# Thirty-two of 88 gate and up tile pairs computed by seven half-width block products instead of eight

## The chip, the cores and the metric

The kernel runs on one core of a Trainium2 chip. The metric is the time on the device, in microseconds (us), of one execution; the median of 3 runs is given. The core has a matrix engine (TensorE, PE in the profile; its weight loads are PEld), VectorE (DVE), ScalarE (ACT), GpSimd (POOL) and SyncE (SP), which here only issues the loads of the weights. Each engine works through its own queue in order and waits on semaphores.

## The reference, cut to what matters

A two-layer network over 512 tokens of width 1024, all float32, then a hybrid mixer and a mixture of experts. Four times in it (two layers, two places each) stands a feed-forward block of hidden width 2816:

```python
def swiglu(h, w_gate, w_up, w_down):
    return (jax.nn.silu(h @ w_gate) * (h @ w_up)) @ w_down

x = x + 0.5 * swiglu(rms_norm(x, norm_w[i, 0]), ffn_w_gate[i, 0], ffn_w_up[i, 0], ffn_w_down[i, 0])
```

## The kernel before, in words

Everything is held transposed: 128 features on the partitions, 512 tokens along the free axis. The stages run in the order ffn00, ssm, ffn01, ffn10, mla, ffn11, mixer, moe; the four that begin with ffn are the blocks above. A float32 product is made from rounded parts: a matrix `a` is split into `a_hi` (rounded) and `a_lo` (the rest), and hi\*hi, hi\*lo and lo\*hi are added up in one PSUM bank, three matmuls of 512 columns for a 128x128 block of weights (`block`, L254 to L256).

A **unit** is eight such blocks of weights (128x1024 numbers, 512 KB). SyncE loads unit `u` into slot `u % 4` of `raw` (in the profile `w_lo_exact`) as soon as TensorE is done with unit `u - 4` (`load_unit`, L224); GpSimd rounds it to `w_hi` (`split_pool`, L232); VectorE makes `w_lo` (`split_vector`, L246); TensorE runs 24 matmuls of 512 columns.

An ffn stage has two halves. A half has eleven **pairs** j = 0 to 10 (`HALF_FF`), each one gate unit and then one up unit, and then eleven units of the down projection, eight output tiles `m` of eleven blocks each. For a pair VectorE scales the gate's sum by the inverse rms (`act`, L738), ScalarE applies silu (L702), VectorE multiplies by the up sum (`prod`, L763), ScalarE rounds the product (`g_hi`, L717), VectorE makes `g_lo` (L770). The hidden product of pair j - 1 and the splits of pair j + 1 are made while TensorE works on pair j. The order of each engine's work is written out by hand, in `ffn_tensor`, `ffn_scalar` and `ffn_vector`, pair by pair.

At the start of a stage ScalarE computes the inverse rms (L318, L320), loads the table for silu (L698) and only then comes to the silu of pair 0. In ffn01 and ffn10 the ScalarE queue also issues, per pair, the load of a piece of another weight (`mod_load`, L798), which waits until VectorE has added the piece before (`mod_add`, L807, two operations per pair).

Of the kernel before, what the change touches and what calls it, by code (L numbers as in the profile page):

```python
# [62 lines left out]
for shared, names in (("lru scalar", ("w hi by scalar", "lru u", "lru gate a", "lru gate x", "lru a", "lru a2", "lru tanh", "root", "gelu")),  # L63
                      ("lru vector", ("lru margin", "lru conv", "log a", "gated x", "one less a2", "lru", "lam", "decay rate", "csp", "slopes")),
# [96 lines left out]
def plan(k):  # L161
# [80 lines left out]
def split_vector(k, u):  # L242

    if u < len(k.units):
        k.ve.wait_ge(*k.at("w hi by scalar" if u in k.by_scalar else "w hi", u))
        k.ve.tensor_tensor(k.w_lo[:, u % SLOTS, :], k.raw[:, u % SLOTS, :], k.w_hi[:, u % SLOTS, :].bitcast(F32), ALU.subtract).then_inc(*k.up("split", u))  # L246


def block(k, u, b, bank, x, first, stop):
# [3 lines left out]
    hi, lo = k.w_hi[:, u % SLOTS, span(b)], k.w_lo[:, u % SLOTS, span(b)]  # L253
# [351 lines left out]
def ffn_tiles(k, with_mod):  # L605
    k.base = k.mod_end_at if with_mod else k.stage_at
    k.g_hi = k.sb("g_hi", [P, HALF_FF, T], F32R)
    k.g_lo = k.sb("g_lo", [P, HALF_FF, T], F32R)
    k.act = k.sb("act", [P, T])
    k.prod = k.sb("prod", [P, T])  # L610
    if with_mod:
        k.mod_w = k.sb("mod_w", [P, 2, 512])
# [11 lines left out]

def ffn_sync(k, stage):
    for u in range(k.unit_at[stage], k.unit_at[stage] + 2 * HALF_UNITS):
        load_unit(k, u)


def ffn_pool(k, stage):  # L630
    u0 = k.unit_at[stage]
# [51 lines left out]

def ffn_scalar(k, stage, mod_tiles=None):
    ae = k.ae
    for half in range(2):
        u0, down = ffn_units(k, stage, half)
        for j in range(HALF_FF):
            if mod_tiles:
# [22 lines left out]
def gate_hi_scalar(k, stage, half, j, down):  # L712
# [4 lines left out]
    ae.activation(k.g_hi[:, j, :], k.prod[:, :], ACT.Copy).then_inc(*k.up("g hi", (stage, half, j)))  # L717


def ffn_vector(k, stage, mod_tiles=None):  # L720
    ve = k.ve
    for half in range(2):
        u0, down = ffn_units(k, stage, half)
        for j in range(HALF_FF):
            if j:
# [23 lines left out]
        for d in range(HALF_FF):  # L749
            split_vector(k, down + d + 2)  # L750
# [6 lines left out]
def gate_prod_vector(k, stage, half, j, u0):  # L757
    ve = k.ve
    ve.wait_ge(*k.at("unit", u0 + 2 * j + 1))
# [3 lines left out]
    ve.tensor_tensor(k.prod[:, :], k.act[:, :], k.bank[UP_BANKS[j % 2]][:, :], ALU.mult).then_inc(*k.up("prod", (stage, half, j)))  # L763


def gate_lo_vector(k, stage, half, j):
# [3 lines left out]
    ve.tensor_tensor(k.g_lo[:, j, :], k.prod[:, :], k.g_hi[:, j, :].bitcast(F32), ALU.subtract).then_inc(*k.up("g lo", (stage, half, j)))  # L770
# [2735 lines left out]
```

## Time and profile before

| | |
|---|---|
| time, median of 3 runs | 2695.33 us (2695.09 to 2696.34) |
| profiled execution, from its first to its last instruction | 2692.5 us |
| matmuls | 12738, TensorE busy 98% |
| VectorE busy | 1632.1 us, 61% |
| ScalarE busy | 869.7 us, 32% |
| GpSimd busy | 653.6 us, 24% |
| mean granted TensorE clock | 0.996 |

The profile gives no other time of that execution than its span, which lies 2.8 us under the median of the runs. A matmul's duration in the profile contains the way through the pipeline, so successive matmuls overlap; what a matmul costs in a dense stretch is the distance from its start to the start of the next. The same holds, by a smaller overlap, for ScalarE and VectorE.

### The profile page before, as it was taken

What the parts mean: (1) busy time and instruction counts of PE and PEld (TensorE: products, weight loads), DVE (VectorE), ACT (ScalarE), POOL (GpSimd) and SP (SyncE); (2) the same over time, 40 slices, a digit from 0 to 9 for tenths busy, and PEclk for the clock granted to TensorE, in tenths of its full rate; (3) what the DMA queues carried; (4) which work ended last, traced back from release to release, by engine and by line L of the source; (5) the groups of instructions that cost most, each with busy time, mean ns of one, the idle gap of its engine ahead of it and who ended that gap; (6) DMA issues with size and microseconds to landing.
All of it is one profiled execution on the core that took longest, in us unless ns stands there. A gap on an engine that the chain in (4) does not pass through costs nothing.

```text
span 2692.5 us, 32765 instructions
## 1 busy us (share of the span) xinstructions
PE 2635.1 (98%) x12738; PEld 2184.7 (81%) x12738; DVE 1632.1 (61%) x2391; ACT 869.7 (32%) x1501; POOL 653.6 (24%) x700
## 2 busy tenths in 40 slices
PE   8999999999999999999999999999999999899998
PEld 6888887778778888888888889988888878777886
DVE  5344468988846545565455657754343477768996
ACT  3101125666611101121001135621001035537995
POOL 2111221222322211221211247722211141012220
PEclk9999999999999999999999999999999999999999
DMA  4333333333324434445445330023333364037995
GB/s 124 98 94 101 95 94 107 96 105 102 94 81 138 141 111 147 133 118 148 125 128 146 104 106 2 9 71 101 94 98 98 92 82 64 15 125 281 373 368 228
DMA packets 457067, 325.80 MB, mean 121 GB/s; under 512 B 34657, under 2 KB 421042, under 8 KB 456658
## 3 DMA queue, kind: packets, MB, share of 16 engines
q1 hardware_dynamic: 435240, 287.22, 36.3%
q10 hardware_dynamic: 15050, 28.08, 3.4%
q0 software_dynamic: 6624, 8.41, 0.9%
q8 instruction: 102, 1.67, 0.3%
q14 instruction: 51, 0.42, 0.0%
HBM read 323.06 MB, written 16.32 MB: 126 GB/s over the span
## 4 chain that ended last, share of the span: by engine, by line
PE 91%; DVE 5%; ACT 2%; DMA 1%; issue 1%; SPq 0%; POOL 0%; DVEq 0%; ACTq 0%; POOLq 0%
PE bank L254 24%; PE bank L256 24%; PE bank L255 24%; PE bank L1483 2%; PE bank L2953 2%; PE bank L2955 1%; PE bank L2954 1%; PE bank L1583 1%; PE bank L1777 1%; PE bank L1789 1%; PE bank L1551 1%; PE bank L2972 1%; PE bank L2974 1%; PE bank L2973 1%; PE bank L2936 1%
## 5 line engine op out<-in xcount | busy, mean ns | idle before, releaser
L254 PE MATMUL bank<-h_hi,w_hi 128*128 128x512 f32 x1992 | 789.6, 396 | 8.5 <-DVE w_lo L246 3.9
L256 PE MATMUL bank<-h_hi,w_lo 128*128 128x512 f32 x1992 | 776.4, 390 | 0.0
L255 PE MATMUL bank<-h_lo,w_hi 128*128 128x512 f32 x1992 | 775.9, 389 | 0.0
L232 POOL TENSOR_SCALAR w_hi<-w_lo_exact 128x1024 fp32r<-128x1024 f32 x325 | 361.9, 1113 | 1464.9 <-DMA w_lo_exact<-in_ffn_w_gate 390.5
L246 DVE TENSOR_TENSOR w_lo<-w_lo_exact,w_hi 128x1024 fp32r<-128x1024 f32 x369 | 455.1, 1234 | 145.1 <-POOL w_hi L232 133.4
L254 PEld LDWEIGHTS bank<-h_hi,w_hi 128*128 128x128 f32 x1992 | 374.2, 188 | 94.9 <-ACT h_hi L350 6.9
L255 PEld LDWEIGHTS bank<-h_lo,w_hi 128*128 128x128 f32 x1992 | 374.4, 188 | 79.3 <-issue 3.4
L256 PEld LDWEIGHTS bank<-h_hi,w_lo 128*128 128x128 f32 x1992 | 374.1, 188 | 78.7
L254 PE MATMUL bank<-g_hi,w_hi 128*128 128x512 f32 x704 | 273.9, 389 | 0.0
L255 PE MATMUL bank<-g_lo,w_hi 128*128 128x512 f32 x704 | 273.9, 389 | 0.0
L256 PE MATMUL bank<-g_hi,w_lo 128*128 128x512 f32 x704 | 273.9, 389 | 0.0
L702 ACT ACTIVATE act<-act 128x512 f32<-128x512 f32 x88 | 55.7, 633 | 629.1 <-DVE act L738 629.0
L738 DVE TENSOR_TENSOR act<-bank,norm_r 128x512 f32<-128x512 f32 x88 | 60.8, 691 | 258.5 <-PE bank L256 235.9
L763 DVE TENSOR_TENSOR prod<-act,bank 128x512 f32<-128x512 f32 x88 | 60.5, 687 | 235.0 <-PE bank L256 233.5
L717 ACT ACTIVATE g_hi<-prod 128x512 fp32r<-128x512 f32 x88 | 55.7, 633 | 402.5 <-DVE prod L763 402.5
L2871 DVE TENSOR_TENSOR e_lo<-e_lo_exact,e_hi 128x1024 fp32r<-128x1024 f32 x138 | 160.7, 1218 | 2.7 <-ACT e_hi L2865 2.7
L254 PEld LDWEIGHTS bank<-g_hi,w_hi 128*128 128x128 f32 x704 | 132.1, 188 | 27.5
L256 PEld LDWEIGHTS bank<-g_hi,w_lo 128*128 128x128 f32 x704 | 132.1, 188 | 27.5
L255 PEld LDWEIGHTS bank<-g_lo,w_hi 128*128 128x128 f32 x704 | 132.1, 188 | 27.3
L2865 ACT ACTIVATE e_hi<-e_lo_exact 128x1024 fp32r<-128x1024 f32 x138 | 138.6, 1060 | 0.9 <-ACT h_rows L3163 0.8
L388 ACT ACTIVATE h_hi<-x,cols 128x512 fp32r<-128x512 f32 x40 | 29.0, 725 | 248.5 <-DVE x L368 153.6
L366 DVE SCALAR_TENSOR_TENSOR norm_ht<-bank,norm_r 128x512 f32<-128x512 f32 x64 | 44.2, 690 | 103.8 <-PE bank L256 103.8
(490 smaller groups left out, 3830.5 us busy)
## 6 DMA issues: line engine op xcount, KB each, us to landing
w_lo_exact<-in_ffn_w_gate SPq DMA_DIRECT2D x88, 512.0 KB, 3.8
w_lo_exact<-in_ffn_w_up SPq DMA_DIRECT2D x88, 512.0 KB, 3.9
w_lo_exact<-in_ssm_w_in SPq DMA_DIRECT2D x48, 512.0 KB, 4.1
mod_w<-in_w_mod ACTq DMA_DIRECT2D x48, 512.0 KB, 3.8
e_lo_exact<-in_w_gate SPq DMA_DIRECT2D x46, 512.0 KB, 6.0
e_lo_exact<-in_w_up SPq DMA_DIRECT2D x46, 512.0 KB, 7.5
e_lo_exact<-in_w_down SPq DMA_DIRECT2D x46, 512.0 KB, 6.6
w_lo_exact<-in_ffn_w_down SPq DMA_DIRECT2D x32, 512.0 KB, 3.9
```

The lines of the kernel that those rows point to most:

```text
L232: ge.tensor_scalar(k.w_hi[:, u % SLOTS, :], k.raw[:, u % SLOTS, :], 1.0, 0.0, ALU.mult, ALU.add).then_inc(*k.up("w hi", u))
L246: k.ve.tensor_tensor(k.w_lo[:, u % SLOTS, :], k.raw[:, u % SLOTS, :], k.w_hi[:, u % SLOTS, :].bitcast(F32), ALU.subtract).then_inc(*k.up(" ...
L254: te.matmul(k.bank[bank][:, :], hi, x_hi, start=first, stop=False)
L255: te.matmul(k.bank[bank][:, :], hi, x_lo, start=False, stop=False)
L256: return te.matmul(k.bank[bank][:, :], lo, x_hi, start=False, stop=stop)
L702: ae.activation(k.act[:, :], k.act[:, :], ACT.Silu).then_inc(*k.up("act", (stage, half, j)))
L717: ae.activation(k.g_hi[:, j, :], k.prod[:, :], ACT.Copy).then_inc(*k.up("g hi", (stage, half, j)))
L738: ve.tensor_tensor(k.act[:, :], k.bank[GATE_BANKS[j % 2]][:, :], k.nr[:, :], ALU.mult).then_inc(*k.up("scaled gate", (stage, half, j)))
L763: ve.tensor_tensor(k.prod[:, :], k.act[:, :], k.bank[UP_BANKS[j % 2]][:, :], ALU.mult).then_inc(*k.up("prod", (stage, half, j)))
L1483: ins = te.matmul(to, w, x, start=m == 0, stop=m == len(terms) - 1)
L2865: ae.activation(k.e_hi[:, n % RING, :], k.e_raw[:, n % RING, :], ACT.Copy).then_inc(*k.up("expert hi", (b, i)))
L2871: ve.tensor_tensor(k.e_lo[:, n % RING, :], k.e_raw[:, n % RING, :], k.e_hi[:, n % RING, :].bitcast(F32), ALU.subtract).then_inc(*k.up("exp ...
```

## The change: what it does

Of the 22 pairs of each ffn stage some are now **joined**: in ffn00 and ffn11 the pairs 4, 6, 7, 9, 10 of the first half and 0, 1, 3, 4, 6, 7, 9, 10 of the second; in ffn01 and ffn10 the pairs 4, 6, 8 of the first half. That is 32 of 88. The others stay as they were.

A joined pair is seen as a 2x2 block product: gate and up are the two block rows, the upper and lower half of the 1024 inputs (four 128-blocks each) the inner index, the first and second 256 tokens the two block columns. It is computed by seven products instead of eight, by a scheme of the Strassen and Winograd family. Each product is 12 matmuls of 256 columns (four blocks, three terms). Three products have quarters of the weights as operands (`UP_1`, `UP_2`, `GATE_2`), four have sums of such quarters (`DIFF`, `SUM`, `SUM_LESS`, `SUM_LEAST`); on the other side stand halves of `h` or four sums of halves, `t`.

New work of VectorE for a joined pair: four sums of quarters (128x512), seven `operand_lo` (128x512), and seven 128x256 operations that put products together and make `prod` in two halves. It makes no 128x1024 splits for it. New work of ScalarE: seven `operand_hi` (128x512) and three copies of products (128x256) out of PSUM. GpSimd no longer rounds the two units of a joined pair. At the start of each ffn stage ScalarE makes `h_exact` (eight 128x512 operations with a scale by column) ahead of the silu of pair 0; in pair 1 VectorE makes four sums `t` and ScalarE their `t_hi` (128x1024 each), in pairs 2 and 3 VectorE makes three and one `t_lo`.

TensorE's order in a joined pair is `UP_1, DIFF, UP_2, SUM, GATE_2, SUM_LESS, SUM_LEAST`. `UP_2`, `GATE_2` and `SUM_LEAST` add onto the PSUM region of `UP_1`, `DIFF` and `SUM`, so each waits until ScalarE has copied that region. A pair now waits for `prod` of the pair two before it, ahead of its first matmul.

The core of the diff:

```diff
 def load_unit(k, u):
     se = k.se
-    if u >= SLOTS:
+    if u - SLOTS in k.joined_units:
+        for name, key in k.joined_units[u - SLOTS]:
+            se.wait_ge(*k.at(name, key))
+    elif u >= SLOTS:
         se.wait_ge(*k.at("unit", u - SLOTS))
...
+def joined_tensor(k, stage, half, j):
...
+    onto = {UP_2: UP_1, GATE_2: DIFF, SUM_LEAST: SUM}
+    for i in range(N_PRODUCTS):
+        te.wait_ge(*k.at("operand lo", (stage, half, j, i)))
+        if i in onto:
+            te.wait_ge(*k.at("copied", (stage, half, j, onto[i])))
...
+        for q in range(KH):
+            x_hi, x_lo = x_of[i](q)
+            te.matmul(out_of[i], hi[:, span(q)], x_hi, start=i not in onto and q == 0, stop=False, skip_group_check=True)
+            te.matmul(out_of[i], hi[:, span(q)], x_lo, start=False, stop=False, skip_group_check=True)
+            ins = te.matmul(out_of[i], lo[:, span(q)], x_hi, start=False, stop=q == KH - 1, skip_group_check=True)
...
+def operand_hi_scalar(k, stage, half, j, i):
...
+    if i in OF_SUMS:
+        ae.wait_ge(*k.at("operand sum", (stage, half, j, i)))
+        source = k.s_exact[:, lo_slot(stage, half, j, i), :]
+    else:
+        u = gate if i == GATE_2 else gate + 1
+        ae.wait_ge(*k.at(f"load {u % SLOTS}", u))
+        source = {UP_1: up_1, UP_2: up_2, GATE_2: gate_2}[i]
+    ae.wait_ge(*k.at(*k.entry_free[stage, half, j, i]))
+    ae.activation(operand_hi(k, stage, half, j, i), source, ACT.Copy).then_inc(*k.up("operand hi", (stage, half, j, i)))
```

ScalarE's queue for pair j (`then`: pair j + 1 is joined; `again`: pairs j and j - 1 are both joined):

```diff
             if (half, j) == (0, 0):
                 exp_tables(k)
                 inverse_rms_scalar(k, stage, D, 7)
                 ae.preload_act_table(ACT.Silu)
+                if stage == "ffn00":
+                    ae.wait_ge(*k.at("x", ("setup", KD - 1)))
+                for m in range(KD):
+                    ae.activation(k.h_exact[:, m, :], k.x[:, m, :], ACT.Copy, scale=gain(k, stage, m)).then_inc(*k.up("h exact", (stage, m)))
+            again = joined and j and is_joined(stage, half, j - 1)
+            if again:
+                operand_hi_scalar(k, stage, half, j, SUM_LESS)
+                ae.wait_ge(*k.at("joined", (stage, half, j - 1, "gate second")))
+                copy_product_scalar(k, stage, half, j, UP_1)
+                copy_product_scalar(k, stage, half, j, DIFF)
+                operand_hi_scalar(k, stage, half, j, SUM_LEAST)
+            if then:
+                operand_hi_scalar(k, stage, half, j + 1, UP_1)
+            if j and is_joined(stage, half, j - 1):
+                silu_scalar(k, stage, half, j - 1)
+            if joined and not again:
+                operand_hi_scalar(k, stage, half, j, SUM_LESS)
+            if j:
+                gate_hi_scalar(k, stage, half, j - 1, down)
...
+            if joined and not again:
...
+                copy_product_scalar(k, stage, half, j, UP_1)
+                copy_product_scalar(k, stage, half, j, DIFF)
+                operand_hi_scalar(k, stage, half, j, SUM_LEAST)
+            if joined:
+                copy_product_scalar(k, stage, half, j, SUM)
+            if then:
+                for i in (SUM, DIFF, UP_2, GATE_2):
+                    operand_hi_scalar(k, stage, half, j + 1, i)
+            if not joined:
+                silu_scalar(k, stage, half, j)
```

VectorE's queue for pair j begins:

```diff
+            if again:
+                operand_lo_vector(k, stage, half, j, SUM)
+                operand_sum_vector(k, stage, half, j, SUM_LEAST)
+                operand_lo_vector(k, stage, half, j, SUM_LESS)
+            if j and is_joined(stage, half, j - 1):
+                joined_rest_vector(k, stage, half, j - 1)
+            if then:
+                operand_sum_vector(k, stage, half, j + 1, SUM)
+            if again:
+                operand_lo_vector(k, stage, half, j, SUM_LEAST)
             if j:
                 gate_prod_vector(k, stage, half, j - 1, u0)
-            if (stage, half, j) != ("ffn00", 0, 0):
-                split_vector(k, u0 + 2 * j + 2)
+            if then:
+                operand_sum_vector(k, stage, half, j + 1, DIFF)
+                operand_lo_vector(k, stage, half, j + 1, UP_1)
+            if joined and not again:
+                operand_lo_vector(k, stage, half, j, SUM)
+                operand_sum_vector(k, stage, half, j, SUM_LEAST)
+                operand_lo_vector(k, stage, half, j, SUM_LESS)
```

## Rows read from the trace of the kernel before

**Rows 1.** The page: busy time of each engine, and the chain that ended last.
```profile
PE 2635.1 (98%) x12738; PEld 2184.7 (81%) x12738; DVE 1632.1 (61%) x2391; ACT 869.7 (32%) x1501; POOL 653.6 (24%) x700
...
PE 91%; DVE 5%; ACT 2%; DMA 1%; issue 1%; SPq 0%; POOL 0%; DVEq 0%; ACTq 0%; POOLq 0%
```
**Rows 2.** Busy time in ffn00's stretch (count), then clock, DMA share, GB/s.
```profile
88.00:388.00 300.00, 300.00 (x1325) 248.43 (x1324) 133.25 (x154) 31.71 (x50) 59.13 (x57) 1.00 0.34 97
```
**Rows 3.** Timeline of SyncE's queue, ffn00: start, duration, what.
```profile
250.02 0.37 SPq L224 DMA_DIRECT2D w_lo_exact<-in_ffn_w_gate  x1
255.46 0.37 SPq L224 DMA_DIRECT2D w_lo_exact<-in_ffn_w_up  x1
```
**Rows 4.** Timeline of GpSimd, same stretch; in brackets the idle time before.
```profile
253.94 1.06 POOL L232 TENSOR_SCALAR w_hi<-w_lo_exact 128x1024 fp32r<-128x1024 f32 x1 [4.10 <-DMA w_lo_exact<-in_ffn_w_gate]
259.31 1.05 POOL L232 TENSOR_SCALAR w_hi<-w_lo_exact 128x1024 fp32r<-128x1024 f32 x1 [4.32 <-DMA w_lo_exact<-in_ffn_w_up]
```
**Rows 5.** Timeline of TensorE in the mixer, matmuls of 256 columns.
```profile
2238.86 0.28 PE L1483 MATMUL bank<-key_hi,query_hi 128*128 128x256 f32 x1
...
2239.82 0.40 PE L254 MATMUL bank<-h_hi,w_hi 128*128 128x512 f32 x1
```
**Rows 6.** Groups of ScalarE by form: busy and mean ns, idle before.
```profile
L3145 ACT ACTIVATE ht_hi<-bank 128x256 fp32r<-128x256 f32 x23 | 8.7, 379 | 1.0 <-PE bank L3044 1.0
```
**Rows 7.** Timeline of ScalarE, two plain operations in the mixer.
```profile
2357.88 0.64 ACT L2528 ACTIVATE norm_acc<-xb 128x512 f32<-128x512 f32 x1
2358.42 0.62 ACT L2536 ACTIVATE norm_sq<-y_last 128x512 f32<-128x512 f32 x1
```
**Rows 8.** Timeline of ScalarE, one scaled by column and the next.
```profile
375.45 0.72 ACT L388 ACTIVATE h_hi<-x,cols 128x512 fp32r<-128x512 f32 x1 [7.12 <-DVE x L368]
376.08 0.61 ACT L391 ACTIVATE norm_sq<-x 128x512 f32<-128x512 f32 x1
```
**Rows 9.** Groups of VectorE by form: an operation of 256 columns.
```profile
L1565 DVE TENSOR_TENSOR turned_lo<-bank,turned_hi 128x256 fp32r<-128x256 f32 x20 | 8.5, 423 | 3.2 <-ACT turned_hi L1560 1.5
```
**Rows 10.** Timeline of VectorE, ffn00, at the end of a pair.
```profile
255.47 0.69 DVE L763 TENSOR_TENSOR prod<-act,bank 128x512 f32<-128x512 f32 x1 [3.61 <-PE bank L256]
256.07 1.22 DVE L246 TENSOR_TENSOR w_lo<-w_lo_exact,w_hi 128x1024 fp32r<-128x1024 f32 x1
257.21 0.68 DVE L770 TENSOR_TENSOR g_lo<-prod,g_hi 128x512 fp32r<-128x512 f32 x1
```
**Rows 11.** Timeline of ScalarE at ffn00's start.
```profile
38.89 1.28 ACT L698 ACT_TABLE_LOAD   x1
```
**Rows 12.** Timeline of VectorE, the same stretch.
```profile
41.52 1.22 DVE L246 TENSOR_TENSOR w_lo<-w_lo_exact,w_hi 128x1024 fp32r<-128x1024 f32 x1
```
**Rows 13.** Timeline of SyncE's queue, the same stretch.
```profile
43.30 0.37 SPq L224 DMA_DIRECT2D w_lo_exact<-in_ffn_w_up  x1
```
**Rows 14.** Timeline of ScalarE in ffn01's first pairs.
```profile
835.20 1.28 ACT L698 ACT_TABLE_LOAD   x1
...
864.39 0.37 ACTq L798 DMA_DIRECT2D mod_w<-in_w_mod  x1
```
**Rows 15.** Timeline of VectorE, the same stretch.
```profile
862.82 1.54 DVE L807 SCALAR_TENSOR_TENSOR mod_acc<-mod_w,c_act,mod_acc 128x512 f32<-128x512 f32 x2
```
**Rows 16.** Timeline of SyncE's queue, the same stretch.
```profile
866.51 0.37 SPq L224 DMA_DIRECT2D w_lo_exact<-in_ffn_w_up  x1
```
**Rows 17.** Stretches of mixer and ssm: busy by engine, then granted clock, DMA, GB/s.
```profile
2306.30:2309.70 3.40, 1.57 (x11) 1.22 (x10) 1.25 (x4) 2.05 (x10) 0.00 (x0) 1.00 0.00 0
2309.70:2313.10 3.40, 3.40 (x16) 3.30 (x15) 2.81 (x9) 3.02 (x7) 0.00 (x0) 0.50 0.00 0
2313.10:2316.50 3.40, 3.40 (x26) 2.89 (x26) 2.26 (x5) 1.07 (x3) 0.00 (x0) 0.99 0.01 2
...
778.40:782.00 3.60, 3.60 (x17) 2.95 (x18) 2.49 (x3) 1.06 (x2) 1.72 (x2) 1.00 0.22 67
```
**Rows 18.** Timeline of TensorE in ssm: a matmul behind idle time (in brackets).
```profile
778.24 0.50 PE L254 MATMUL bank<-y_hi,w_hi 128*128 128x512 f32 x1 [2.06 <-DVE x L364]
```

More of the change, by code:

```diff
@@ L602 @@
         "mixer": "moe"}
[L605 to L612, printed above, removed]
 HALF_UNITS = 3 * HALF_FF
 LAST_UNIT = [(m * HALF_FF + HALF_FF - 1) // KD for m in range(KD)]
-GATE_BANKS, UP_BANKS, DOWN_BANKS = (0, 1), (2, 3), (4, 5)
+GATE_BANKS, UP_BANKS, DOWN_BANKS = (0, 2), (1, 3), (4, 5)
+JOINED = {"ffn00": ((4, 6, 7, 9, 10), (0, 1, 3, 4, 6, 7, 9, 10)), "ffn11": ((4, 6, 7, 9, 10), (0, 1, 3, 4, 6, 7, 9, 10)), "ffn01": ((4, 6, 8), ()), "ffn10": ((4, 6, 8), ())}
+KH, HALF_T, QUARTER = KD // 2, T // 2, KD // 2 * P
+LO_SLOTS, HI_SLOTS = {"ffn00": 14, "ffn01": 6, "ffn10": 6, "ffn11": 14}, 2 * SLOTS
+N_PRODUCTS = 7
+UP_1, DIFF, UP_2, SUM, GATE_2, SUM_LESS, SUM_LEAST = range(N_PRODUCTS)
+OF_WEIGHTS, OF_SUMS = (UP_1, UP_2, GATE_2), (DIFF, SUM, SUM_LESS, SUM_LEAST)
+ACROSS, BELOW, LAST, SECOND = range(4)
 def ffn_units(k, stage, half):
@@ L625, in ffn_sync, with operand_hi @@
+def operand_hi(k, stage, half, j, i):
+    at = k.entry_at[stage, half, j, i]
+    return k.w_hi[:, at // 2, at % 2 * QUARTER:(at % 2 + 1) * QUARTER]
 def ffn_sync(k, stage):
@@ L687, in ffn_scalar @@
         u0, down = ffn_units(k, stage, half)
+        if half and is_joined(stage, 1, 0):
+            for i in (UP_1, SUM, DIFF, UP_2, GATE_2):
+                operand_hi_scalar(k, stage, 1, 0, i)
         for j in range(HALF_FF):
+            joined, then = is_joined(stage, half, j), j + 1 < HALF_FF and is_joined(stage, half, j + 1)
             if mod_tiles:
@@ new lines, in t_lo_vector, with two_less_vector, joined_sums_vector @@
+def t_lo_vector(k, stage, n):
+    ve = k.ve
+    ve.wait_ge(*k.at("t hi", (stage, n)))
+    ve.tensor_tensor(k.t_lo[n], k.t_exact[n], k.t_hi[n].bitcast(F32), ALU.subtract).then_inc(*k.up("t lo", (stage, n)))
+def two_less_vector(k, stage, half, j):
+    ve = k.ve
+    ve.wait_ge(*k.at("copied", (stage, half, j, SUM)))
+    ve.tensor_tensor(k.two_less, k.copies[DIFF], k.copies[SUM], ALU.subtract).then_inc(*k.up("two less", (stage, half, j)))
+def joined_sums_vector(k, stage, half, j):
+    ve = k.ve
+    right = k.bank[UP_BANKS[j % 2]]
+    ve.wait_ge(*k.at("product", (stage, half, j, SUM_LESS)))
+    ve.wait_ge(*k.at("copied", (stage, half, j, UP_1)))
+    ve.tensor_tensor(k.first_sum, right[:, HALF_T:T], k.copies[UP_1], ALU.add).then_inc(*k.up("joined", (stage, half, j, "first")))
+    ve.wait_ge(*k.last("joined"))
+    ve.wait_ge(*k.last("prod"))
+    ve.tensor_tensor(k.act[:, 0:HALF_T], right[:, 0:HALF_T], k.first_sum, ALU.add).then_inc(*k.up("joined", (stage, half, j, "gate first")))
+    ve.wait_ge(*k.at("two less", (stage, half, j)))
+    ve.tensor_tensor(k.act[:, HALF_T:T], k.first_sum, k.two_less, ALU.add).then_inc(*k.up("joined", (stage, half, j, "gate second")))
@@ L749, in ffn_vector @@
         for d in range(HALF_FF):
-            split_vector(k, down + d + 2)
+            u = down + d + 2
+            if half or d < HALF_FF - 2 or not is_joined(stage, 1, 0):
+                split_vector(k, u)
+            else:
+                first_sums = (SUM, DIFF) if d == HALF_FF - 2 else (SUM_LESS,)
+                for i in first_sums:
+                    operand_sum_vector(k, stage, 1, 0, i)
+                for i in (UP_1, DIFF) if d == HALF_FF - 2 else (UP_2, GATE_2):
+                    operand_lo_vector(k, stage, 1, 0, i)
             for m in range(KD):
@@ L758, in gate_prod_vector @@
     ve = k.ve
[L759 removed]
+    up = k.bank[(GATE_BANKS if is_joined(stage, half, j) else UP_BANKS)[j % 2]]
+    if not is_joined(stage, half, j):
+        ve.wait_ge(*k.at("unit", u0 + 2 * j + 1))
     ve.wait_ge(*k.at("act", (stage, half, j)))
```

262 lines of the change are left out of this document (237 added, 25 removed).

## The prediction

> **What bounds the kernel now.** I read the page first. TensorE is busy for 98% of the span and makes 91% of the chain; VectorE is at 61%, ScalarE at 32% [rows 1]. A busy matmul engine alone proves little, so I then asked for its busy time in ffn00 alone: 300.00 of 300.00 us, with ScalarE at 32 and VectorE at 133 us [rows 2]. No other engine keeps it waiting there. Next come the queues beside it. SyncE issues a load the moment a unit is released, every 5.44 us [rows 3]: 24 matmuls, so 0.227 us each, and a pair costs 10.88 us. GpSimd starts on the loaded unit 3.92 and 3.85 us after such an issue [rows 3, 4]. So the second unit of a pair whose slot is freed at the end of a pair arrives some 3.9 us into the next; before, that was early enough by half a pair. The reader should keep this number: what the change does to TensorE's work is plain, what it does to the order of waits is not.
>
> **TensorE's own work.** A joined pair is 7 x 12 = 84 matmuls of 256 columns for 48 of 512. The nearest row for 256 columns is a dense run in the mixer with fresh weights for each matmul: eight starts in 2239.82 - 2238.86 = 0.96 us, 0.120 us each [rows 5], more than half of 0.227, which is 0.113. I take 0.120 in the sum and keep 0.113 as the lower bound. A product is then 12 x 0.120 = 1.44 us, a pair 10.08 us, and the saving 0.80 us; over 32 pairs **-25.6 us**. At 0.113 it is 1.36 us a product, 9.52 a pair, 1.36 saved, -43.5 in all. The Trainium skill ("TensorE: Matmul & The Clock Gate", Back-to-back issue gap) has 262 cycles for 256 columns, about 109 ns; by that 84 matmuls would take 9.2 us and the saving would be 54 us. The measured 0.120 and 0.227 are both above its figures (it has 518 cycles, 216 ns, for 512 columns), so the rows decide.
>
> **ScalarE and VectorE per joined pair.** One plain 128x512 operation costs ScalarE 2358.42 - 2357.88 = 0.54 us of its queue [rows 7], though it lasts 0.63; a copy of 256 columns lasts 0.38 [rows 6]. VectorE pays 256.07 - 255.47 = 0.60 us for 512 columns and 257.21 - 256.07 = 1.14 for 1024 [rows 10]; 256 columns last 0.42 [rows 9], and less the same overlap of 0.09 cost 0.33. A joined pair has 13 operations of 512 columns (four sums, seven lows, the scaled gate, g_lo) and seven of 256 on VectorE: 7.8 + 2.3 = 10.1 us, as much as TensorE's 10.08; on ScalarE nine of 512 and three of about 0.3, 5.8 us. An ordinary pair has 2 x 1.14 + 3 x 0.60 = 4.1 us on VectorE. Two joined and one ordinary make 24.3 of 31.0 us, so VectorE has room on average; the question is in which order its and ScalarE's queues meet the late load.
>
> **The wait that the change adds.** Take pair 5 ordinary, 6 and 7 joined. Zero is the release of the up unit of pair 5. That frees the slot for the up unit of pair 7, which lands at about 3.95 (3.9 from above, and a wake-up). While TensorE does pair 6, ScalarE's queue begins with `operand_hi` of `UP_1` of pair 7, which waits for this load. Behind it stand, in this order, `operand_hi` of `SUM_LESS` of 6, `g_hi` of 5 and the copy of `UP_1` of 6. They start at 3.95, 4.49, 5.03 and 5.57; the copy ends at 5.95 and TensorE may start `UP_2` at 6.0. `UP_1` and `DIFF` were done with 2 x 1.44 us of work; without the wait `UP_2` would have started 0.19 before 2.88, at 2.7. TensorE stands for **3.3 us**. After that the rest keeps up. VectorE's queue is blocked by the same load (`DIFF` of 7), then makes the lows and the last sum of 6 at 5.4 to 8.6, ahead of TensorE, which reaches `SUM` at 7.4 and `SUM_LESS` at 10.3. It ends the sums of 6 about 1 us into pair 7, and pair 7 frees its operands early, so pairs 7 and 8 run without a gap.
>
> This holds wherever a joined pair follows an ordinary one and is followed by a joined one: pairs 6, 9 of the first half and 3, 6, 9 of the second, in ffn00 and ffn11: 10 x 3.3 = 33 us. Pair 0 of the second half has no `g_hi` ahead of the copy, which starts at 5.03: 2.8 us, twice, 5.6. The lone pairs 4 and 8, and 6 in ffn01 and ffn10, have no joined pair behind them and do not wait. Together **+38.6 us**: a two-of-three group of three pairs costs 10.88 + 10.08 + 3.3 + 10.08 = 34.3 us against 32.6. The bounds come from the load: at 3.6 or 4.2 us to landing it is 4 us less or more.
>
> **The start of a stage.** Eight scaled operations go ahead of silu, at 376.08 - 375.45 = 0.63 us [rows 8], 5.0 us. In ffn00 the table load ends at 40.17 [rows 11], silu of pair 0 then at 45.85 and `prod` at 46.6; the split of the gate of pair 2, started at 41.52 before [rows 12], stands behind `prod` in VectorE's queue and ends at 47.7. The pair before is released at 43.30, so its successor could start at 43.1 [rows 13]: **+4.7 us**. In ffn01 the table load ends at 836.48 [rows 14]; the same chain ends at 844.1, and TensorE gets there at 844.6, so nothing is lost. But VectorE then works without a pause from 842.2: pair 1 has 4.1 + 4.6 (the sums `t`) + 1.5 (`mod_add`, [rows 15]), pair 2 has 4.1 + 3.4 + 1.5, pair 3 has 6.0 (ten operations for pairs 2, 3 and 4) + 1.1 + 1.5: 27.8 us, until 870.0. Pair 4 begins at 866.5 [rows 16]. Its `mod_load` stands first in ScalarE's queue and waits for that, 3.5 us in; with 0.37 for the issue [rows 14] and two operations the copy of `UP_1` ends at 5.4, and TensorE loses 2.7. ffn10 is alike: **+5.4 us**. ffn11 has no `mod_add` and is clear. This term could be 0 to 8.
>
> The splits that GpSimd and VectorE drop, and the loads, which are the same bytes, cost nothing and gain nothing, for TensorE covers them [rows 2].
>
> **The clock.** That makes 15 stands of 2.7 to 4.7 us. The clock column shows what idling can do: in the mixer TensorE was busy for 1.57 of 3.4 us, and the next 3.4 us were granted 0.50, 1.2 for 2.4 GHz, then full speed again [rows 17]. An idle piece of 2.06 us at 778 [rows 18] was followed by no fall, the stretch behind it has 1.00 [rows 17]. A half-speed piece costs 3.4 / 2 = 1.7 us of work. Bounds are 0 and 15 x 1.7 = 25; as my stands are longer than the one that cost nothing, I take half, **+12 us**. The skill's same page (HAM oscillation) says that idle gaps between bursts of matmuls bring the slow clock back; that speaks for the upper half.
>
> **Sum.** -25.6 + 38.6 + 4.7 + 5.4 + 12 = +35.1 us on the span of 2692.5. The median of the runs is 2.8 above the span, which I take as kept: 2695.3 + 35 = **2730 us**.
>
> **Rivals.**
> 1. *No wait to speak of.* If ScalarE's late load does not reach TensorE, say since the slot of the up unit comes free sooner than I read it, only work and starts are left: -25.6 + 4.7 + 5.4 = -15.5, 2680 us; at 0.113 it is 2662. It decides from a landing under 0.6 us after the release, for then the copy ends by 2.7. Against it: the release is SyncE's wait for that very unit, and every load took over 3.8 us [rows 3, 4]. Chance 0.12.
> 2. *Narrow matmuls at half the price of wide ones.* 0.113 us each: the waits grow by 0.16 us to 40.5, the net is -43.5 + 40.5 + 10.1 = +7, with the clock term +19: 2714 us, or 2702 without. For it: my 0.120 comes from runs of other tiles. The skill's 262 cycles, above, would go further, by 11 us. Chance 0.18.
> 3. *VectorE becomes the bound.* If each of its operations costs its whole duration (0.69, 0.42), a joined pair has 9.0 + 2.9 = 11.9 us, the group of three 29 of 34: it still fits, but pair 6's sums end some 2.5 us into pair 7 and the copies behind them come 1 us late, 12 times: 2742 us. Chance 0.10.
> 4. The forecast itself, 0.60, with its own range of 2716 to 2746: clock term 0 to 25, starts 0 to 8 off.
>
> **The numbers.** A change under 0.2%, 5.4 us, is about what a measurement of this kernel cannot tell. Faster is rival 1, 0.12. Same, 0.04, is the part of rival 2 with a steady clock and short starts. Slower is the rest, 0.84. The range leaves out most of rival 1 and the tails: 2702 to 2750.
>
> **What would show it.** Right: in the profile after, TensorE has idle time of about 3.3 us ahead of the first matmul of `UP_2` in pairs 3, 6 and 9, put down to ScalarE's copy; that copy starts right behind an `operand_hi` that waited for the up load; 84 matmuls of a joined pair at 0.120 us without a gap in pairs 7 and 10; 4.7 us ahead of the third gate of ffn00; clock digits under 9 in ffn00 and ffn11. Wrong: if the waits sit at `operand_lo` the bound is VectorE; if TensorE runs through at 0.12 the load was not late, and the kernel is faster.

## The result, and the profile after

The changed kernel takes 2762 us (four executions, 2758.24 to 2764.09, median 2762.04; with the fifth, below, the median is 2762.63), against 2695.09 for five executions of the kernel before: ratio 1.0244 [1.0231, 1.0258], slower. The forecast of 2730 had the direction and half of the size; the time lies 12 us above the range. (The fifth execution took 14882 us and is left out; the profile shown here is therefore of a second set of runs of the same kernel, `after_again`, median 2763.64 us, ratio 1.0255 [1.0238, 1.0272].) Before that profile was taken, 2758 to 2765 us were expected of it, 49 us of stands, and 44 us lost to the clock; the time and the places came so, the stands have 53.3 us, and the clock, as worked out below, 28.1 in the four stages.

The page of the changed kernel, the lines that answer to [rows 1]:

```profile
span 2762.4 us, 36643 instructions
...
PE 2642.5 (96%) x13890; PEld 2244.4 (81%) x13890; DVE 1900.0 (69%) x2903; ACT 1059.8 (38%) x1869; POOL 599.0 (22%) x636
...
PE 81%; DVE 8%; DMA 4%; ACT 4%; issue 2%; POOL 0%; SPq 0%; ACTq 0%; DVEq 0%; POOLq 0%
```

TensorE's part of the chain falls from 91% to 81%; what it lost went to VectorE, DMA and ScalarE. The profile's mean granted clock is 0.984, against 0.996. The same stretch of ffn00 as in [rows 2], with the columns of that group:

```profile
88.00:388.00 300.00, 276.94 (x1653) 250.13 (x1652) 197.87 (x312) 80.14 (x156) 34.11 (x29) 0.97 0.31 90
```

Before, 300.00 of 300.00 us were busy, at clock 1.00. Now 23 us are idle, and the mean clock of the stretch is 0.97. Those are the two things to follow. The waits of TensorE in the whole run (total, times, longest), the first lines:

```profile
PE bank L808 <- DVE s_lo L986: 34.8, 10, 3.7
PE bank L266 <- DVE w_lo L258: 15.4, 12, 4.5
PE bank L808 <- ACT norm_ht L884: 14.6, 5, 4.4
```

L808 is the first matmul of a narrow product. The first group names VectorE's `s_lo` (the low part of an operand), the third ScalarE's copy: `UP_2` waits for several semaphores, and the profile names one. VectorE around pair 6 of ffn00's first half:

```profile
87.71 1.29 DVE L986 TENSOR_TENSOR s_lo<-w_lo_exact,w_hi 128x512 fp32r<-128x512 f32 x2
...
97.36 0.69 DVE L986 TENSOR_TENSOR s_lo<-s_lo_exact,w_hi 128x512 fp32r<-128x512 f32 x1
```

By the order of the code the first row holds the low parts of `UP_2` and `GATE_2` of pair 6, done at 89.0. The second is that of `SUM`; it ends at 98.05, when the copy does too, but `UP_2` does not wait for it. So it was the copy, and reading the first group as "VectorE is the bound" would have been a mistake. ScalarE at pair 6 of ffn00's first half:

```profile
96.09 0.63 ACT L877 ACTIVATE w_hi<-w_lo_exact 128x512 fp32r<-128x512 f32 x1 [8.24 <-DMA w_lo_exact<-in_ffn_w_up]
96.63 0.61 ACT L877 ACTIVATE w_hi<-s_lo_exact 128x512 fp32r<-128x512 f32 x1
97.15 0.61 ACT L971 ACTIVATE g_hi<-norm_sq 128x512 fp32r<-128x512 f32 x1
97.67 0.64 ACT L884 ACTIVATE norm_ht<-bank 128x256 f32<-128x256 f32 x2
```

and SyncE, TensorE in the same stretch:

```profile
91.93 0.37 SPq L234 DMA_DIRECT2D w_lo_exact<-in_ffn_w_up  x1
```
```profile
93.05 0.28 PE L810 MATMUL bank<-h_hi,s_lo 128*128 128x256 f32 x1
...
94.49 0.28 PE L810 MATMUL bank<-t_hi,s_lo 128*128 128x256 f32 x1
98.17 0.36 PE L808 MATMUL bank<-h_hi,w_hi 128*128 128x256 f32 x1 [3.40 <-DVE s_lo L986]
```

This is the chain of the forecast, link by link: the load of `UP_1` of pair 7 is issued at 91.93, ScalarE has waited 8.24 us when it begins with it at 96.09, the sum, `g_hi` and the copies follow at 0.52 to 0.54 us each, the first copy is done near 98.05, and TensorE starts `UP_2` at 98.17, 3.40 us late. The last matmuls of two products lie 94.49 - 93.05 = 1.44 us apart, twelve at 0.120.

What the forecast had too small: the clock, which falls in the middle of ffn00. Windows around pair 6 of the second half (columns as in [rows 17]), and the matmul that ended the stand:

```profile
286.00:291.00 5.00, 2.74 (x23) 2.53 (x22) 1.57 (x3) 0.98 (x2) 0.00 (x0) 1.00 0.76 209
291.00:297.80 6.80, 5.69 (x27) 5.72 (x28) 4.08 (x7) 2.06 (x6) 0.00 (x0) 0.50 0.29 82
297.80:304.60 6.80, 6.80 (x58) 6.80 (x58) 5.40 (x11) 3.29 (x7) 0.00 (x0) 1.00 0.26 77
```
```profile
292.11 0.55 PE L808 MATMUL bank<-h_hi,w_hi 128*128 128x256 f32 x1 [3.37 <-DVE s_lo L986]
```

0.50 is 1.2 of 2.4 GHz: 27 matmuls in 6.8 us, 1.1 of it idle, then 58. The rows that the forecast used have such a piece as 3.4 us [rows 17]; here it is 6.8.

And waits at a place that the forecast had called free, behind the first down unit of ffn00's first half. TensorE, GpSimd, VectorE:

```profile
153.39 0.47 PE L266 MATMUL bank<-g_hi,w_hi 128*128 128x512 f32 x1 [1.18 <-DVE w_lo L258]
...
162.16 0.50 PE L266 MATMUL bank<-g_hi,w_hi 128*128 128x512 f32 x1 [1.69 <-DVE g_lo L1145]
```
```profile
150.93 1.05 POOL L244 TENSOR_SCALAR w_hi<-w_lo_exact 128x1024 fp32r<-128x1024 f32 x1 [38.36 <-PE bank L810]
152.37 4.77 POOL L244 TENSOR_SCALAR w_hi<-w_lo_exact 128x1024 fp32r<-128x1024 f32 x3 [0.39 <-PE bank L810]
```
```profile
152.02 1.22 DVE L258 TENSOR_TENSOR w_lo<-w_lo_exact,w_hi 128x1024 fp32r<-128x1024 f32 x1 [3.28 <-POOL w_hi L244]
154.19 2.05 DVE L258 TENSOR_TENSOR w_lo<-w_lo_exact,w_hi 128x1024 fp32r<-128x1024 f32 x1 [0.94 <-POOL w_hi L244]
```

GpSimd splits four down units at once, and begins only at 150.93, after L810, a matmul of the last pair's products. The ring of eight half-slots of `w_hi` explains it: a joined pair takes eight entries (seven products and one skipped), an ordinary pair four. Ahead of the down units `plan_joined` brings the count `e` back to the slots that it would have without joined pairs, with `e += (2 * down - e) % HI_SLOTS`. Each joined pair has taken four entries more than an ordinary one, so with an odd number of them in a half this skips four entries, and the splits of the first down units wait for operands of the very last pair. All four stages have such a first half (5 or 3 joined pairs); the second halves have 8 or none and no such wait.

### The profile page after: what moved, and what is told of

Its sections match the earlier page's. It is cut to its first block, busy times and chain, and to the rows that moved or that the text cites. A ratio compares the mean times of both kernels' runs of the same rounds, so it can differ in the third digit from the quotient of the medians.

```text
span 14881.2 us, 36643 instructions
## 1 busy us (share of the span) xinstructions
PE 14869.9 (100%) x13890; PEld 11051.6 (74%) x13890; DVE 1877.9 (13%) x2903; ACT 1086.2 (7%) x1869; POOL 554.5 (4%) x636
## 4 chain that ended last, share of the span: by engine, by line
PE 100%; DMA 0%; ACT 0%; DVE 0%; POOL 0%; issue 0%; POOLq 0%
PE bank L266 22%; PE bank L268 22%; PE bank L267 22%; PE bank L810 4%; PE bank L809 4%; PE bank L808 4%; PE bank L1858 2%; PE bank L1958 2%; PE bank L3328 2%; PE bank L3330 2%; PE bank L3329 2%; PE bank L2152 1%; PE bank L305 1%; PE bank L2164 1%; PE bank L1926 1%; PE bank L3347 1%
## 5 line engine op out<-in xcount | busy, mean ns | idle before, releaser
L266 PE MATMUL bank<-h_hi,w_hi 128*128 128x512 f32 x1480 | 2572.0, 1738 | 0.0
L268 PE MATMUL bank<-h_hi,w_lo 128*128 128x512 f32 x1480 | 2508.6, 1695 | 0.0
L267 PE MATMUL bank<-h_lo,w_hi 128*128 128x512 f32 x1480 | 2507.3, 1694 | 0.0
L267 PEld LDWEIGHTS bank<-h_lo,w_hi 128*128 128x128 f32 x1480 | 1350.7, 913 | 607.3 <-issue 607.3
L268 PEld LDWEIGHTS bank<-h_hi,w_lo 128*128 128x128 f32 x1480 | 1352.5, 914 | 603.5 <-issue 603.5
L266 PEld LDWEIGHTS bank<-h_hi,w_hi 128*128 128x128 f32 x1480 | 1348.0, 911 | 608.5 <-issue 608.4
L267 PE MATMUL bank<-g_lo,w_hi 128*128 128x512 f32 x704 | 1193.0, 1695 | 0.0
L268 PE MATMUL bank<-g_hi,w_lo 128*128 128x512 f32 x704 | 1192.8, 1694 | 0.0
L266 PE MATMUL bank<-g_hi,w_hi 128*128 128x512 f32 x704 | 1192.5, 1694 | 0.0
L268 PEld LDWEIGHTS bank<-g_hi,w_lo 128*128 128x128 f32 x704 | 643.1, 913 | 287.2 <-issue 287.2
L810 PE MATMUL bank<-t_hi,s_lo 128*128 128x256 f32 x488 | 505.7, 1036 | 0.0
L808 PE MATMUL bank<-t_hi,w_hi 128*128 128x256 f32 x488 | 504.3, 1033 | 0.0
L810 PEld LDWEIGHTS bank<-t_hi,s_lo 128*128 128x128 f32 x488 | 461.8, 946 | 0.0
L808 PEld LDWEIGHTS bank<-t_hi,w_hi 128*128 128x128 f32 x488 | 461.0, 945 | 0.0
L808 PE MATMUL bank<-h_hi,w_hi 128*128 128x256 f32 x384 | 396.2, 1032 | 0.0
```

The lines of the kernel that those rows point to most:

```text
L266: te.matmul(k.bank[bank][:, :], hi, x_hi, start=first, stop=False)
L267: te.matmul(k.bank[bank][:, :], hi, x_lo, start=False, stop=False)
L268: return te.matmul(k.bank[bank][:, :], lo, x_hi, start=False, stop=stop)
L808: te.matmul(out_of[i], hi[:, span(q)], x_hi, start=i not in onto and q == 0, stop=False, skip_group_check=True)
L810: ins = te.matmul(out_of[i], lo[:, span(q)], x_hi, start=False, stop=q == KH - 1, skip_group_check=True)
```

## The experiments

Times are medians; ratios are against the kernel before, run on the same chip beside them (its medians 2694.8 to 2695.7). Edits are against the changed kernel.

**1. The chain's own test, `own_first`.** In a joined pair that follows an ordinary one, ScalarE and VectorE do the pair's own copies and operands before they wait for the next pair's load:

```diff
-            if then:
+            own_first = joined and not again
+            if then and not own_first:
                 operand_hi_scalar(k, stage, half, j + 1, UP_1)
...
                 operand_hi_scalar(k, stage, half, j, SUM_LEAST)
+            if then and own_first:
+                operand_hi_scalar(k, stage, half, j + 1, UP_1)
```

and likewise on VectorE the sum `DIFF` and the low part of `UP_1` of the next pair behind the low part of `SUM_LEAST`.

> In a joined pair that follows an ordinary one and precedes a joined one, ScalarE's operand_hi of UP_1 and VectorE's DIFF and UP_1 operations of the next pair go behind the pair's own copies and operands. Late-load theory: the twelve stands go, 39 us, and with them twelve of fifteen chances for the clock to fall, about 35 us: 2688 us, give or take 10. VectorE theory: its queue is as long as before, so only a part goes, and the time stays above 2740 us.

Measured: 2701.41 us, ratio 1.0027 [1.0017, 1.0036], 62 us less than the changed kernel. TensorE at the same place:

```profile
93.88 0.28 PE L810 MATMUL bank<-t_hi,s_lo 128*128 128x256 f32 x1
94.00 0.28 PE L808 MATMUL bank<-h_hi,w_hi 128*128 128x256 f32 x1
```

`UP_2` follows the product before it after 0.12 us; all twelve stands are gone. Left are 4.50 us at the start of ffn00, 4.33 us in pair 4 of ffn01 and of ffn10, 11.9 us at the down units, and four falls of the clock inside the stages instead of eleven. By the trace the twelve stands (40.1 us) and the clock time that went with them (28.1 - 7.8 = 20.3 us, worked out below) make 60.4 us, for 59.4 between the two spans and 62 between the medians. The 13 us by which it missed its expectation of 2688 are the clock: that took 35 us for the falls, where 20.3 came back.

The edit moves both queues, and no run moves one alone. From the rows above, ScalarE's order alone would not have been enough, by my estimate: `SUM` would then have been due near 96.1, and its low part, behind the same load in VectorE's queue, ended at 98.05.

**2. The stands without the idleness, `filler`.** The same waits, but TensorE does 14 matmuls of 512 columns on a bank that nobody reads, ahead of `UP_2` in the pairs that stood (12 in pair 0); their results are thrown away.

```diff
+            if i == UP_2 and j + 1 < HALF_FF and is_joined(stage, half, j + 1) and not (j and is_joined(stage, half, j - 1)):
+                busy_tensor(k, 6, 14 if j else 14 - 2)
             te.wait_ge(*k.at("copied", (stage, half, j, onto[i])))
```

> The changed kernel with 14 matmuls of 512 columns (12 in pair 0) on an unused bank ahead of UP_2 where the late load makes TensorE stand; they take the 3.2 us that it stands for, and the output is the same. Clock follows idleness: the waits stay, but twelve of fifteen falls go, about 35 us: 2727 us, mean clock over 0.99. Rival, the clock falls for the narrow matmuls themselves and not for the stands: time and clock as before, 2762 us and 0.984.

Measured: 2746.26 us, ratio 1.0187 [1.0170, 1.0204], 17.4 us less, though the time of the stands is still spent. At the place of the fall shown above the windows now read:

```profile
291.00:297.80 6.80, 6.80 (x59) 6.80 (x58) 5.21 (x11) 3.48 (x7) 0.00 (x0) 1.00 0.39 117
297.80:304.60 6.80, 6.80 (x59) 6.80 (x59) 5.71 (x9) 2.96 (x6) 2.10 (x2) 1.00 0.27 77
```

Falls inside the four stages are left only where there is no filler: at 45.0 (start of ffn00), and at 891.5 and 1263.5 (pair 4 of ffn01 and ffn10). So the falls come from the stands, and not from the narrow matmuls, which are all still there. The falls in the four stages now cost 6.7 us for 28.1, so 21.4 came back; the two spans differ by 16.7, since a fall in ssm (1.7) and small waits elsewhere took part of it again. The expectation of 2727 took the whole step down to 0.984 as theirs; the kernel before has 0.996 itself, so it was too large.

**3. The scaled operations behind the first silu, `h_late`.** The eight `h_exact` operations move behind `silu_scalar` of pair 0.

```diff
...
-                for m in range(KD):
-                    ae.activation(k.h_exact[:, m, :], k.x[:, m, :], ACT.Copy, ...
...
                 silu_scalar(k, stage, half, j)
+            if (half, j) == (0, 0):
...
+                for m in range(KD):
+                    ae.activation(k.h_exact[:, m, :], k.x[:, m, :], ACT.Copy, ...
```

> The eight h_exact operations go behind the silu of pair 0 in ScalarE's queue. Late-load theory: the 4.7 us at the third gate of ffn00 go, and the 5.4 us in pair 4 of ffn01 and ffn10, since VectorE is no longer 3.5 us late there, and three falls of the clock, 9 us: 2743 us. Rival, the starts are hidden anyway: 2760 us.

Measured: 2754.12 us, ratio 1.0223 [1.0206, 1.024], 9.5 less. The stand of 4.52 at ffn00's start is gone, but two waits of 0.7 us at most at the start and one of 1.91 in pair 4 of that half are new, and pair 4 of ffn01 and ffn10 still stands, 3.81 and 2.61 us for 4.35 and 4.33. That is half of the expected gain. The start's work was moved, not removed; that TensorE, no longer held up at the start, now reaches pair 4 before VectorE is ready is my reading of it, and was not tested.

**4. Both edits together, `both`.**

> own_first and h_late together. Late-load theory with three further waits found in the last profiles: own_first ran at 2701 with a 4.5 us stand at ffn00's third gate, 4.3 us in pair 4 of ffn01 and ffn10 and four pairs of waits in the down projection of a half with an odd number of joined pairs (1.2 and 1.7, 0.65 and 2.4 us). h_late takes the first and some of the second: 2691 us, 0.1 to 0.2% under the kernel before. Rival, VectorE is still short in the two-of-three groups: 2700 us.

Measured: 2697.88 us, ratio 1.0007 [0.9998, 1.0016]: no difference from before, and 7 us above the expectation. Here 32 joined pairs are worked in seven products each and nothing is gained, since 7.4 us of stands in pair 4, 11.9 at the down units, 1.5 at the start of ffn00 and five falls of 3.4 us (8.0 us lost) take it back. The rival's time, 2700, is nearer than the 2691 of the late-load theory, but its cause is not in the trace: TensorE has no stand in the pairs of the two-of-three groups beyond pair 4.

**5. An even number of joined pairs in every half, `even`.** Both edits, and four pairs fewer:

```diff
-JOINED = {"ffn00": ((4, 6, 7, 9, 10), (0, 1, 3, 4, 6, 7, 9, 10)), ..., "ffn01": ((4, 6, 8), ()), ...
+JOINED = {"ffn00": ((6, 7, 9, 10), (0, 1, 3, 4, 6, 7, 9, 10)), ..., "ffn01": ((6, 8), ()), ...
```

(ffn11 as ffn00, ffn10 as ffn01; 28 joined pairs.) This drops pair 4 of every first half, where `mod_add` is late, and leaves no skipped entries ahead of the down units.

> As both, but with an even number of joined pairs in each half: (6, 7, 9, 10) in the first half of ffn00 and ffn11, (6, 8) in ffn01 and ffn10, 28 joined in all. A joined pair takes eight half-slots of w_hi and an ordinary one four, so an odd number leaves four to be skipped before the down projection, and the split of its second unit must then wait for the last up unit. Theory: the waits in the down projection go (11.7 us and their falls of the clock), and so does the stand in pair 4, which is no longer joined (4 to 8 us), for four savings of 0.8 lost: 2695 - 28 x 0.8 + 1 = 2674 us. Rival, those waits come from VectorE's load and not from the slots: over 2685 us.

Measured: **2675.5 us**, ratio 0.9925 [0.9912, 0.9939]: 20.2 us faster than the kernel before, and the fastest that was run. Its page, and the windows of ffn00 from 88 to 376:

```profile
PE 2615.7 (98%) x13746; PEld 2214.8 (83%) x13746; DVE 1872.7 (70%) x2843; ACT 1041.9 (39%) x1829; POOL 602.9 (23%) x644
```
```profile
88.00:376.00 288.00, 288.00 (x1745) 259.09 (x1744) 210.83 (x327) 87.36 (x164) 38.16 (x36) 1.00 0.36 101
```

TensorE is busy without a pause at clock 1.00, and issues 1745 matmuls. There is no fall of the clock in the four stages. 28 x 0.80 = 22.4 us less 2.1 of new waits (0.58 and 1.49 at ffn00's start) make 20.3, for 20.2 between the medians. That the two agree so closely is partly luck, for the profiled spans differ by 18.2: mixer and moe, which the change does not touch, differ between the two executions too. Cleaner is the second half of ffn00, with eight joined pairs and no wait. From the last matmul of the down units before it to the first of the down units behind its pairs it takes 311.90 - 198.34 = 113.56 us, before 320.55 - 200.64 = 119.91: 6.35 less, 0.79 per pair, for 0.80 forecast.

**6. No pair joined, `none_late`, and lone pairs only, `lone_late`.** `JOINED` empty, or 20 joined pairs of which no two are neighbours (4, 6, 8, 10 and 1, 3, 5, 7 in ffn00 and ffn11; 6, 8 in ffn01 and ffn10), both with `h_late`.

> No pair joined, h_late; h_exact, the sums t and their splits are still made and read by no one. Theory: hidden in ScalarE's and VectorE's idle time, 2695 us, within 3. Rival, they cost at the start of each stage: 2700 us or more.

> h_late with 20 joined pairs of which no two are neighbours, an even number in each half: (4, 6, 8, 10) and (1, 3, 5, 7) in ffn00 and ffn11, (6, 8) in ffn01 and ffn10. No pair waits for the load of the one after next. Price theory: 20 x 0.80 us less than none_late, 2679 us; at 0.113 us for a matmul it would be 20 x 1.36, 2668. Rival, each joined pair costs a stand of its own: above 2685.

Measured: 2700.21 us, 1.0018 [1.0009, 1.0028], and 2682.14 us, 0.995 [0.9935, 0.9965]. The difference is 18.1 us, 0.90 per joined pair against 0.80 forecast; the two intervals leave 0.7 to 1.1. Of the twenty joined pairs, each with ordinary ones on both sides, nineteen cost no stand, as the forecast said; pair 4 of ffn00 has one of 1.93 us. Nothing joined is 4.5 us slower than the kernel before, 5 above the expectation; its profile has two new waits at ffn00's start, 0.58 and 1.52 us, which cover the 1.6 us by which its span of 2694.1 is longer. The rest of the 4.5 is in no profile and stays open.

**7. The skip moved, `pad_alone`, `front_pad`, `front_pad_5`.** The four skipped half-slots go ahead of pair 2, where GpSimd seemed to have time to spare, instead of ahead of the down units:

```diff
                 gate, up = u0 + 2 * j, u0 + 2 * j + 1
+                if j == 2:
+                    e += 4 * (len(JOINED[stage][half]) % 2)
```

`pad_alone` has this edit alone, `front_pad` with both others and all 32 pairs, and `front_pad_5` besides has 5, 7, 9 joined in ffn01 and ffn10 instead of 4, 6, 8.

> The changed kernel with one edit: in a half with an odd number of joined pairs the four half-slots of w_hi that are skipped to bring the ring back in step are skipped ahead of pair 2 and not ahead of the down projection. Slot theory: the waits behind the first down units go, 11.8 us in all in the profile, with no fall of the clock among them: 2752 us. Rival, they come from how much VectorE has to do at the end of a half: no change, 2764 us.

Measured: 2746.46 us, ratio 1.0191 [1.0174, 1.0208], 17.2 less than the changed kernel. TensorE's waits from 140 to 165 in the changed kernel are

```profile
PE bank L266 <- DVE g_lo L1145: 1.7, 1, 1.7
PE bank L266 <- DVE w_lo L258: 1.2, 1, 1.2
```

and there is none in that stretch here: one edit of the plan removes the four pairs of waits, 11.8 us. It is not quite free: waits of 0.4, 0.4 and 0.6 us in the first half of ffn01, ffn10 and ffn11 have grown to 1.3, 1.6 and 1.4, 2.9 together. And this execution lost 22.5 us to falls for 28.1 (one fall more, but ten of the twelve only 3.4 us long). That makes -11.8 + 2.9 - 5.6 = -14.5, for -15.0 between the two spans. The fifteen stands themselves kept their size, as its first waits of the whole run show beside those above:

```profile
PE bank L810 <- DVE s_lo L988: 34.4, 10, 3.8
PE bank L810 <- ACT norm_ht L886: 15.4, 5, 4.3
PE bank L266 <- DVE w_lo L258: 11.6, 8, 4.5
```

> The same edit in both (own_first and h_late), all 32 pairs joined. Slot theory: 2697.9 less 11.9 us of waits and 3.4 of two falls of the clock: 2683 us. Left are 1.9 us in pair 4 of ffn00 and 2.9 and 2.6 in ffn01 and ffn10 with three falls. Rival: no change, 2698 us.

> As front_pad, with pairs 5, 7, 9 joined in ffn01 and ffn10 for 4, 6, 8. VectorE is behind in pair 4 since it makes the sums t beside mod_add; a pair later it has caught up. Theory: 5.5 us of waits and 3.4 of two falls go, 2675 us. Rival, mod_load holds ScalarE's queue in any joined pair: no change against front_pad.

Measured: 2688.15 us, 0.9974 [0.9965, 0.9984], and 2680.89 us, 0.9948 [0.9932, 0.9965]. Both are faster than the kernel before, though 5 and 6 us above their expectations. `front_pad` is slower than `even`; of `front_pad_5` that is hardly shown, since its interval and that of `even` overlap. In `front_pad` pair 4 of ffn01 and of ffn10 stands longer than in `both`, 4.33 and 4.36 us for 2.93 and 2.58, with a fall of 6.8 us each; the shift of the joined pairs by one in `front_pad_5` takes 7.3 us of that off. No kernel with 32 joined pairs had a median under that with 28, so in the orders tried here the four pairs that `even` drops did not bring in their 3.2 us of work.

## Why the prediction was right and wrong

By its own steps, the forecast and what the trace of the changed kernel has. Forecast span: 2692.5 + 35.1 = 2727.6. Measured: 2762.4, +69.9.

| step of the forecast | forecast | measured |
|---|---|---|
| TensorE's own work, 32 x 0.80 | -25.6 | -25.6 (0.120 us each) |
| late load, twelve stands | +38.6 | +40.1 |
| start of ffn00 | +4.7 | +4.5 |
| pair 4 of ffn01 and ffn10 | +5.4 | +8.7 |
| splits at the down units | 0 | +11.8 |
| one small wait in ffn11 | not named | +0.6 |
| clock | +12 | +28.1 |
| sum | +35.1 | +68.2 |

1.7 us of the 69.9 stay unassigned.

**TensorE's own work: right.** 0.120 us for 256 columns held in the place of use, and `even` and the pair of `none_late` and `lone_late` give it back in whole kernels (0.72 and 0.90 us a pair, the first with its stands, for 0.80; 0.79 in a stretch without any). Rival 2 (0.113) falls. Two slips of the prediction change nothing here: its 54 us by the Trainium skill ("TensorE: Matmul & The Clock Gate", Back-to-back issue gap) set that page's narrow matmul against a wide one of the trace, while both of its figures, 262 and 518 cycles, give an estimated 38 us, and the trace 25.6; and the group of three in rival 3 takes VectorE 28.3 us, not 29.

**The wait that the change adds: right, in mechanism, place and size.** Twelve stands of 2.63 to 3.75 us; the ten forecast at 3.3 have 3.16 to 3.75, the two forecast at 2.8 have 2.63 and 2.75. At pair 6 above, `UP_2` starts 2.08 us after ScalarE gets the load (96.09 to 98.17), for 2.05 in the forecast; the load came 4.16 us after its issue, for 3.95. `own_first` takes them all away by order alone, with the same loads, slots and operations, which shows that it was the order of the queues. Rivals 1 and 3 fall: the load is late, VectorE at 69% ended none of the twelve, and its operations start 0.60 us apart in the same timeline (97.36 and 97.96), so they do not cost their whole 0.69.

**The clock: the largest failing step.** The prediction said: "A half-speed piece costs 3.4 / 2 = 1.7 us of work. Bounds are 0 and 15 x 1.7 = 25; as my stands are longer than the one that cost nothing, I take half, +12 us." Both factors were too small. Of the 15 stands of 2.6 to 4.5 us that it named, 11 were followed by a fall, not half; four were not, at 98.2, 221.0, 2046.5 and 2081.4. And eight of the eleven lasted 6.8 us, not 3.4:

| fall begins, lasts | stand that it belongs to, ends |
|---|---|
| 45.3, 6.8 | 4.52, 46.04 |
| 134.0, 3.4 | 3.75, 133.21 |
| 256.9, 3.4 | 3.69, 255.97 |
| 291.0, 6.8 | 3.37, 292.11 |
| 328.6, 6.8 | 3.35, 329.26 |
| 898.6, 6.8 | 4.35, 900.37 |
| 1267.2, 6.8 | 4.33, 1269.06 |
| 1919.2, 6.8 | 3.16, 1919.84 |
| 1956.7, 6.8 | 3.58, 1957.41 |
| 2117.1, 3.4 | 3.34, 2115.98 |
| 2151.3, 6.8 | 3.58, 2152.32 |

That is 64.9 us at half speed. In 8.6 of them TensorE was standing, which costs nothing twice; the other 56.2 us did 28.1 us of work, so 28.1 were lost. The kernel before has no fall in these stages. The forecast's upper bound, 25, lies under that, because it took one fall of 3.4 us [rows 17] for the length of all. The trace of before holds a longer one, which the forecast did not look for; its window, beyond the mixer:

```profile
2425.80:2432.60 6.80, 6.80 (x24) 5.83 (x24) 5.44 (x23) 5.37 (x7) 0.00 (x0) 0.50 0.58 233
```

In this execution the sorting is clean: the eight falls that began while TensorE still stood lasted 6.8 us, the three that began after it had started again lasted 3.4. The length of the stand does not sort them (3.35 and 3.34 us are on either side). A shift of the program changes all of it: `pad_alone`, with the same fifteen stands, has twelve falls, ten of them 3.4 us, and two of these ten began 0.4 and 0.3 us before the stand's end, so the sorting is no rule. `filler` shows that the falls follow from the stands. The Trainium skill ("TensorE: Matmul & The Clock Gate", HAM oscillation) says that idle gaps between bursts of matmuls bring the slow clock back; by it I should have taken the upper half, and the trace agrees with it in 11 of 15 places.

**The splits: wrong.** "The splits that GpSimd and VectorE drop, and the loads ... cost nothing and gain nothing, for TensorE covers them." That looked at their work and not at when their slots come free. 11.8 us in eight waits of 0.65 to 2.4 us; that the skip is the cause is shown by `pad_alone`, which moves it and has none of the eight. The diff held all that was needed: a joined pair takes four entries of the ring more than an ordinary one, the ring has eight, and an odd number of fours leaves a half ring to skip.

**The start of a stage: right in ffn00** (4.52 for 4.7), and in ffn01 and ffn10 right in place but too small, 4.35 and 4.33 us for 2.7:

```profile
896.12 2.18 DVE L1182 SCALAR_TENSOR_TENSOR mod_acc<-mod_w,c_act,mod_acc 128x512 f32<-128x512 f32 x2
```
```profile
898.33 0.38 ACTq L1173 DMA_DIRECT2D mod_w<-in_w_mod  x1
898.81 0.63 ACT L877 ACTIVATE w_hi<-s_lo_exact 128x512 fp32r<-128x512 f32 x1 [4.88 <-DVE mod_acc L1182]
899.35 0.61 ACT L971 ACTIVATE g_hi<-norm_sq 128x512 fp32r<-128x512 f32 x1
899.87 0.64 ACT L884 ACTIVATE norm_ht<-bank 128x256 f32<-128x256 f32 x2
```

The chain is the forecast's (ScalarE's `mod_load` waits for VectorE's `mod_add`, and the copy stands behind it), but `mod_acc` ends at 898.30, and its two operations take 2.18 us, for 1.54 in [rows 15]: so VectorE came later than the forecast's sum of durations had it. 0.64 us of the 1.6 are this row; where the other came from, I did not separate.

So the forecast came out 35 us of span too low: clock 16.1, down units 11.8, pair 4 3.3, late loads 1.5, a small wait less the start 0.4, unassigned 1.7. The clock alone would have left the time inside the range (2730 + 16 = 2746, under 2750); it took the down units, put at nothing, as well to carry it out. The slower verdict rested on the first large term, the late load, and that held.

## What to carry to other kernels

Before an operation with a wait goes to the front of an in-order queue, ask what is queued behind it that somebody needs sooner: here moving two lines of ScalarE's and VectorE's order took 62 us back. Where a change alters how many entries a piece of work takes in a ring, count the entries to the next reuse and see whether the last piece before the boundary and the first behind it now share them. And price a stand of a few us on TensorE with its clock: in these stages fifteen stands of 53.3 us together cost 28.1 more, about half as much again. The way out that is shown is to remove the stand: one that was only shortened or moved to 1.9 us still had a fall behind it in three runs of five (last section).

## What the hardware showed that was not expected

- The granted clock fell for 3.4 us or for 6.8 us (1.2 of 2.4 GHz both times), after stands of 2.6 to 4.5 us. In other runs stands of 1.9 us in pair 4 of ffn00 had a fall of 3.4 us behind them (`both`, `front_pad`, `front_pad_5`), or none (`h_late`, `lone_late`).
- Stands of the same length fell on both sides: 3.40 us at 98.2 had no fall behind it, 3.37 us at 292.1 had 6.8 us.
- VectorE's operations take longer beside GpSimd's splits in some places: 2.05 us for a `w_lo` of 1024 columns, 1.52 us for a `g_lo` of 512, against 1.22 and 0.68 us [rows 10]. In the changed kernel at ffn00's start, VectorE and GpSimd:

```profile
44.68 1.22 DVE L258 TENSOR_TENSOR w_lo<-w_lo_exact,w_hi 128x1024 fp32r<-128x1024 f32 x1
45.81 1.52 DVE L1145 TENSOR_TENSOR g_lo<-norm_sq,g_hi 128x512 fp32r<-128x512 f32 x1
```
```profile
45.36 1.44 POOL L244 TENSOR_SCALAR w_hi<-w_lo_exact 128x1024 fp32r<-128x1024 f32 x1 [7.43 <-DMA w_lo_exact<-in_ffn_w_up]
```

The split runs from 45.36 to 46.80. The `w_lo` that began before it keeps its 1.22 us; the `g_lo` that began behind it takes more than twice its time and ends 0.53 us after the split, which itself takes 1.44 us for 1.06 [rows 4]. `mod_acc` at 896.12 has a split beside it as well. That the two engines' sharing of something is the cause was not tested.
